# A hybrid-attention stage on one core: the compressed blocks' projections come first, their steps lie between the other units, and the two full branches run alone at the end

## What is computed

```python
def hybrid_mixer(h, w_in, gk_up, gk_bias, gla_norm, cmp_pe, cmp_w1, cmp_w2, w_out):
    q_a, k_a, v_a, lr_a, r_a, q_b, kv_b, g_b = split_cols(h @ w_in, HYB_SPLITS)
    o_a = gla_mixer(q_a, k_a, v_a, lr_a, r_a, gk_up, gk_bias, gla_norm)
    o_b = nsa_mixer(q_b, kv_b, g_b, cmp_pe, cmp_w1, cmp_w2)
    return jnp.concatenate([o_a, o_b], axis=-1).astype(h.dtype) @ w_out
...
    def compress(a, j):                      # nsa_mixer: 15 overlapping blocks of 32 tokens
        blocks = a[:, :, blk_idx] + cmp_pe[j]
        h = jax.nn.gelu(blocks.reshape(B, G, n_cmp, CMP_BLOCK * Dh) @ cmp_w1[j])
        return h @ cmp_w2[j]
...
        o = gb[..., 0:1] * o_cmp + gb[..., 1:2] * o_slc + gb[..., 2:3] * o_win
```

## Time and profile before

| | us |
|---|---|
| median of 3 runs | 2643.16 |
| the profiled execution, its own time | 2645.73 |
| its span in the trace | 2643.9 |
| projections, from the first matmul to the first score `S` of a full branch | 45.12 to 157.15 |
| attention, to the first `ul_hyb_out` | 157.15 to 260.37 |
| output product and the sum into X, about | 260.4 to 298 |

### The profile page before, as it was taken

How to read it: one execution, slowest core, us unless ns; L and a number is a source line. 1 busy time by engine, 2 the same in 40 slices (tenths; PEclk the granted TensorE clock), 3 DMA queues, 4 the chain that set the end, 5 groups by cost and what they waited for, 6 DMA issues and landing times.

```text
span 2643.9 us, 32969 instructions
## 1 busy us (share of the span) xinstructions
PE 2432.2 (92%) x13898; PEld 2108.3 (80%) x13898; DVE 1984.5 (75%) x2208; ACT 1431.7 (54%) x1594; POOL 209.3 (8%) x261
## 2 busy tenths in 40 slices
PE   4877899898889999999999999998897999897998
PEld 3756799787777888888888888887887997886997
DVE  6756777686657898888888989886666775767675
ACT  3312443464546776767676767674444653344562
POOL 1101001000000000000000000001311110221110
PEclk8886899897889999999999999999998999998999
DMA  9652678432256999999999999995224453323552
GB/s 318 216 196 88 215 271 302 158 139 81 96 182 232 348 360 347 358 348 360 352 356 337 369 338 367 342 365 191 69 96 159 164 190 134 108 76 118 195 184 77
DMA packets 263558, 608.44 MB, mean 230 GB/s; under 512 B 18472, under 2 KB 33082, under 8 KB 263402
## 3 DMA queue, kind: packets, MB, share of 16 engines
q1 hardware_dynamic: 247808, 554.39, 58.4%
q0 software_dynamic: 14640, 51.49, 5.8%
q10 hardware_dynamic: 954, 0.37, 0.1%
HBM read 605.17 MB, written 1.05 MB: 229 GB/s over the span
## 4 chain that ended last, share of the span: by engine, by line
PE 80%; DVE 10%; ACT 5%; DMA 2%; issue 1%; POOL 1%; SPq 0%; PEldq 0%; PEld 0%; DVEq 0%; ACTq 0%; POOLq 0%
PE ps L132 78%; PE ps L136 2%; DVE eb L153 1%; DMA slots<-in_hyb_mod_w 1%; DVE X L153 1%; ACT L142 1%; DMA beside<-in_dense_mod_w 1%; DVE ul_in L145 1%; DVE macc L153 1%; DVE xn L153 1%; ACT uh_ffn L139 0%; ACT eb L139 0%; ACT xn L139 0%; DVE ul_ssm_w L145 0%; DVE gate L153 0%
## 5 line engine op out<-in xcount | busy, mean ns | idle before, releaser
L145 DVE TENSOR_TENSOR ul_moe_w<-slots,uh_moe_w 128x2048 fp32r<-128x2048 f32 x334 | 762.6, 2290 | 108.7 <-ACT uh_moe_w L139 108.4
L139 ACT ACTIVATE uh_moe_w<-slots 128x2048 fp32r<-128x2048 f32 x334 | 640.2, 1917 | 215.8 <-PE ps L132 187.4
L132 PE MATMUL ps<-uh_moe_w,XGh 128*128 128x512 f32 x896 | 356.7, 398 | 3.1 <-DVE XGl L145 2.1
L132 PE MATMUL ps<-uh_moe_w,XGl 128*128 128x512 f32 x896 | 349.5, 390 | 0.0
L132 PE MATMUL ps<-ul_moe_w,XGh 128*128 128x512 f32 x896 | 349.0, 389 | 0.0
L145 DVE TENSOR_TENSOR ul_ffn<-slots,uh_ffn 128x2048 fp32r<-128x2048 f32 x62 | 142.1, 2292 | 101.1 <-ACT uh_ffn L139 101.1
L132 PE MATMUL ps<-HTf,uh_ffn 128*128 128x256 f32 x704 | 201.5, 286 | 2.8 <-DVE HTlf L145 2.8
L132 PE MATMUL ps<-HTlf,uh_ffn 128*128 128x256 f32 x704 | 201.0, 285 | 0.0
L132 PE MATMUL ps<-HTf,ul_ffn 128*128 128x256 f32 x704 | 200.9, 285 | 0.0
L132 PEld LDWEIGHTS ps<-uh_moe_w,XGh 128*128 128x128 f32 x896 | 168.3, 188 | 39.1 <-DVE XGl L145 2.2
L132 PEld LDWEIGHTS ps<-uh_moe_w,XGl 128*128 128x128 f32 x896 | 168.2, 188 | 35.8
(11 more groups left out here) (509 smaller groups left out, 5576.4 us busy)
## 6 DMA issues: line engine op xcount, KB each, us to landing
slots<-in_moe_w_gu SPq DMA_DIRECT2D x111, 2048.0 KB, 8.8
slots<-in_moe_w_down SPq DMA_DIRECT2D x56, 2048.0 KB, 7.9
slots<-in_w_up SPq DMA_DIRECT2D x20, 2048.0 KB, 7.9
slots<-in_w_in SPq DMA_DIRECT2D x14, 2048.0 KB, 8.5
slots<-in_dense_w_gu SPq DMA_DIRECT2D x10, 2048.0 KB, 9.9
slots<-in_ssm_w_in SPq DMA_DIRECT2D x10, 2048.0 KB, 8.0
slots<-in_w_down SPq DMA_DIRECT2D x10, 2048.0 KB, 7.8
slots<-in_dense_w_down SPq DMA_DIRECT2D x5, 2048.0 KB, 12.7
```

The source lines that it names most:

```text
L132: return self.e.matmul(o, lhsT, rhs, start=start, stop=stop, skip_group_check=skip) if self.e else DONE
L139: return self.e.activation(o, i, f, **kw) if self.e else DONE
L145: return self.e.tensor_tensor(o, a, b, op) if self.e else DONE
```

## The change

The units of the compressed blocks' input (`hyb_c`) come first and their first-layer weights (`hyb_w1`) are loaded third and fifth. The compressed branch leaves the woven part: its generators are created before the projections' loop and `beside` takes one step of them behind the tile and GLA piece of given steps n. Three GLA pieces move by two steps. Banks and buffers are divided anew: `mix` takes the place of `xn`, `nb0` gets its own buffer, and `bkc` (the bank of the compressed branch) has one bank. The multiplication with the gate (`facc`) moves behind the arrival of `gt`. The branches alone are woven at the end.

```diff
-    mix = c.sb("mix", [128, 2, D], ph)
+    mix = xn
...
-    units = [Unit("hyb_r", (KC, 528), slice(0, KC), slice(0, 16), False)] + row_units("hyb_r", 528, 16, 2)
+    units = column_units("hyb_c", 256, 128)
+    units += [Unit("hyb_r", (KC, 528), slice(0, KC), slice(0, 16), False)] + row_units("hyb_r", 528, 16, 2)
     units += column_units("hyb_qk", 512, 128) + row_units("hyb_v", 512, 0, 2) + column_units("hyb_q", 512, 128)
-    units += column_units("hyb_c", 256, 128) + column_units("hyb_kv", 256, 128) + column_units("hyb_kw", 280, 128)
+    units += column_units("hyb_kv", 256, 128) + column_units("hyb_kw", 280, 128)
...
-    bk1, bk2, bs = c.pool(range(4)), c.pool(range(4, 7)), c.pool([7])
-    bkc, bkb = c.pool(range(5, 7)), [c.pool(range(0, 3)), c.pool(range(3, 5))]
+    bk1, bk2, bkc, bs = c.pool(range(4)), c.pool(range(4, 6)), c.pool([6]), c.pool([7])
+    bkb = [c.pool(range(0, 3)), c.pool(range(3, 6))]
...
-    LR, R, QK, V, Q, C, KV0, KV1, GT = 0, 1, 5, 9, 13, 17, 19, 21, 23
+    C, LR, R, QK, V, Q, KV0, KV1, GT = 0, 2, 3, 7, 11, 15, 19, 21, 23
...
     def sync(e):
+        def compressing(j):
+            c.load(e, ("hyb_w1", j), io["nsa_cmp_w1"][0][j].rearrange("(i p) n -> p i n", p=128), (16, 256))
+
+        c.columns(e, "hyb_c", W, 2064, 256)
         c.columns(e, "hyb_r", W, 1024, 528)
+        compressing(0)
         c.columns(e, "hyb_qk", W, 0, 512)
+        compressing(1)
         c.columns(e, "hyb_v", W, 512, 512)
         c.load(e, "hyb_q", None, (KC, 512), heads)
-        c.columns(e, "hyb_c", W, 2064, 256)
         c.columns(e, "hyb_kv", W, 2320, 256)
         c.columns(e, "hyb_kw", W, 2576, 280)
-        for j in range(2):
-            c.load(e, ("hyb_w1", j), io["nsa_cmp_w1"][0][j].rearrange("(i p) n -> p i n", p=128), (16, 256))
...
-    Z, GATES, SCALED, STATE, INSIDE, OUTER, NORM = 6, 7, 10, 14, 17, 19, 23
+    Z, GATES, SCALED, STATE, INSIDE, OUTER, NORM = 6, 7, 12, 16, 19, 21, 25
...
-    def blocks(e, hf, compressed, rest):
-        if hf == 0:
-            yield from compressed(e)
-        else:
-            for _ in range(8):
-                yield
-        yield from rest(e, hf)
+    COMPRESSED, BLOCKS = (5, 11, 13, 14, 15, 16, 17), (21, 22, 23, 25)
+
+    def beside(n, compressed, *halves):
+
+        if n in COMPRESSED:
+            next(compressed, None)
+        if n in BLOCKS:
+            for half in halves:
+                next(half, None)
...
-        e.tensor_tensor(facc[:, :], smc[:, :], gt[:, hf, :].rearrange("p (a c) -> p c a", c=3)[:, 0, :], ALU.mult).then_inc(*v.up(("facc", hf)))
...
         ps = c.psum.of(("nsa_oc", hf))
+        e.wait_ge(*v.at("gt"))
+        e.tensor_tensor(facc[:, :], smc[:, :], gt[:, hf, :].rearrange("p (a c) -> p c a", c=3)[:, 0, :], ALU.mult).then_inc(*v.up(("facc", hf)))
...
     def tensor(e):
         c.side_banks = bs
+        small_parts = compressed_tensor(e), blocks_tensor(e, 0), blocks_tensor(e, 1)
         e.wait_ge(*v.at(("HT", 7)))
         for n in range(NU + AHEAD):
...
             gla_tensor(e, n)
+            beside(n, *small_parts)
         S.t.mark("in_end")
-        weave(branch_tensor(e, 0), branch_tensor(e, 1), blocks(e, 0, compressed_tensor, blocks_tensor), blocks(e, 1, None, blocks_tensor))
+        weave(branch_tensor(e, 0), branch_tensor(e, 1))
```

More of the change, by code:

```diff
@@ L1052, in hybrid @@
     pe2 = c.sb("pe2", [128, 2, 16], ph)
-    ph.close()
     gla_landed, nsa_landed = c.event_signal("gla_consts_landed", 16), c.event_signal("nsa_consts_landed", 16)
-    pg = c.above(86)
-    hT, hTl = c.sb("HT0", [128, KC, T], pg, R32), c.sb("HTl0", [128, KC, T], pg, R32)
-    units = [Unit("hyb_r", (KC, 528), slice(0, KC), slice(0, 16), False)] + row_units("hyb_r", 528, 16, 2)
-    units += column_units("hyb_qk", 512, 128) + row_units("hyb_v", 512, 0, 2) + column_units("hyb_q", 512, 128)
-    units += column_units("hyb_c", 256, 128) + column_units("hyb_kv", 256, 128) + column_units("hyb_kw", 280, 128)
[L1061 to L1074, removed]
+    pg = ExitStack()
     Sb = [c.sb(f"S{i}", [128, 8, 256], pg) for i in range(2)]
@@ L1079, in hybrid @@
     facb = [c.sb(f"fac{i}", [128, 8], pg) for i in range(2)]
-    small = [[c.sb(f"c{n}{i}", sh, pg) for n, sh in (("s", [128, 8, 16]), ("m", [128, 8]), ("u", [128, 8]), ("f", [128, 8]), ("p", [128, 128]), ("t", [128, 128]))] for i in range(2)]
     pg.close()
-    mh, ml = c.put(44, "mixTh", [128, 8, T], R32), c.put(52, "mixTl", [128, 8, T], R32)
+    hT, hTl = c.sb("HT0", [128, KC, T], ph, R32), c.sb("HTl0", [128, KC, T], ph, R32)
+    units = column_units("hyb_c", 256, 128)
+    units += [Unit("hyb_r", (KC, 528), slice(0, KC), slice(0, 16), False)] + row_units("hyb_r", 528, 16, 2)
+    units += column_units("hyb_qk", 512, 128) + row_units("hyb_v", 512, 0, 2) + column_units("hyb_q", 512, 128)
+    units += column_units("hyb_kv", 256, 128) + column_units("hyb_kw", 280, 128)
+    U = Units(S, "in", units, 1024, ph)
+    vT = [c.sb(f"vT{i}", [128, T], ph) for i in range(2)]
+    hid = c.sb("hid", [128, 2, 2, 2, 16], ph)
+    hx = c.sb("hx", [30, 2, 256], ph)
+    px = ExitStack()
+    xk = c.sb("xk", [128, 2, 16, 30], px)
+    px.close()
+    hy, hz = c.sb("hy", [30, 2, 256], ph), c.sb("hz", [30, 2, 256], ph)
+    kcT = c.sb("kcT", [128, 16], ph)
+    vbd = c.sb("vbd", [128, 8, 64], ph)
+    hrep = c.sb("hrep", [128, 2, 8, 16], ph)
+    vct = c.sb("vct", [128, 64], ph)
+    small = [[c.sb(f"c{n}{i}", sh, ph) for n, sh in (("s", [128, 8, 16]), ("m", [128, 8]), ("u", [128, 8]), ("f", [128, 8]), ("p", [128, 128]), ("t", [128, 128]))] for i in range(2)]
+    nb = [c.sb("nb0", [128, 2, 512], ph), Og[:, :, :, :].rearrange("p g a v -> p g (a v)")]
+    ph.close()
+    mh, ml = c.put(36, "mixTh", [128, 8, T], R32), c.put(44, "mixTl", [128, 8, T], R32)
     O = Units(S, "out", tile_units(("hyb_out", 0), 4, 1) + tile_units(("hyb_out", 4), 4, 1), 1024,
-              buffers=[c.put(at, f"u{n}_hyb_out", [128, 3, 1024], R32) for n, at in (("h", 60), ("l", 72))])
-    bk1, bk2, bs = c.pool(range(4)), c.pool(range(4, 7)), c.pool([7])
-    bkc, bkb = c.pool(range(5, 7)), [c.pool(range(0, 3)), c.pool(range(3, 5))]
+              buffers=[c.put(at, f"u{n}_hyb_out", [128, 3, 1024], R32) for n, at in (("h", 52), ("l", 64))])
+    bk1, bk2, bkc, bs = c.pool(range(4)), c.pool(range(4, 6)), c.pool([6]), c.pool([7])
+    bkb = [c.pool(range(0, 3)), c.pool(range(3, 6))]
     bt, bs2 = c.pool(range(3)), c.pool([3])
@@ L1121, in gpsimd @@
             e.dma_start(w2[:, j, :, :], io["nsa_cmp_w2"][0][j].rearrange("(c p) d -> p c d", p=128)).then_inc(*nsa_landed.up("consts"))
+        e.memset(hid[:, :, :, :, :].rearrange("p a b c d -> p (a b c d)"), 0.0).then_inc(*g.up("hid0"))
         c.follow(e, "hyb_in")
         S.g.mark("in_end")
-        S.wait_for(e, "in_end")
-        e.memset(hid[:, :, :, :, :].rearrange("p a b c d -> p (a b c d)"), 0.0).then_inc(*g.up("hid0"))
         c.follow(e, "hyb_attention")
@@ L1169, in tile_tensor @@
         U.used(n)
-        if C <= n < KV0:
+        if C <= n < LR:
             j = n - C
@@ L1233, in tile_vector @@
             c.psum.leave(("hyb_tile", n), v)
-        elif C <= n < KV0:
+        elif C <= n < LR:
             j = n - C
@@ L1437, in compressed_tensor @@
         c.side_t.step()
-        for _ in range(3):
-            yield
+        yield
         for j in range(2):
@@ L1473, in compressed_scalar @@
         e.activation(hz[:, :, :], hy[:, :, :], AF.Exp, scale=-2.0 * 0.7978845608028654).then_inc(*a.up("gelu"))
-        for _ in range(6):
+        for _ in range(4):
             yield
@@ L1758, in scalar @@
         U.split_hi(e, 1)
+        small_parts = compressed_scalar(e), blocks_scalar(e, 0), blocks_scalar(e, 1)
         for n in range(AHEAD, NU + AHEAD):
@@ L1784, in vector @@
         U.split_lo(e, 1)
+        small_parts = compressed_vector(e), blocks_vector(e, 0), blocks_vector(e, 1)
         for n in range(AHEAD, NU + AHEAD):
```

8 lines of the change are left out of this document (4 added, 4 removed).

## The result

| | before | after |
|---|---|---|
| median of 7 runs, us | 2642.9 (2632.05 to 2646.93) | 2658.42 (2653.31 to 2662.03) |
| ratio of the runs, 95% interval | | 1.006 (1.004 to 1.0081) |
| profiled execution: its time, span | 2645.73, 2643.9 | 2662.03, 2660.2 |
| first `S` of a branch | 157.15 | 215.54 |
| first `ul_hyb_out` | 260.29 | 269.06 |

The first `ul_hyb_out` before starts at 260.29; the table ahead of the prediction has it 0.08 us too late. One execution of the later run with the steps by engine and two banks took 4004.5 us at a granted clock of 0.56, where its others had 0.95; it counts in that run's median and not in its ratio.

The account below looks back on a forecast made before the run. Attention was taken as bound by chains between engines, projections by PE with DVE close behind. Projections +52 and attention -48 us gave +4, about 2650 us profiled and 2647 us median, range 2635 to 2659.

Parts of the forecast that it names:

- Two of the named signs: Profile signs in the projections: `hx` shows 6.4 to 9 us twice; second `vbd` product's bank wait is 10 us or more.
- The attention: Attention without the compressed branch: branches alone take 55 us, giving back 48 us, bounds 45 and 51.
- 1 and 2, the moved products: Compressed-branch products laid between projection units on PE: two `hx` add 13.6 us, the small ones 7.5 us.
- 3, the waits: Projections: PE waits that nothing covers, for tiles DVE must treat first, at steps 5 to 23; sum 19.2 us.
- Rival B: Projections: DVE runs ahead and waits are covered better than counted, so faster, 2635 us; chance 0.22.
- 4, the end: Projections' end: gates, whole norm, table load, `cf`/`nb` pairs and first scores before the first `S`, 13.4 against 5.5: +7.9 us.
- 5, the clock: Projections: new waits and crowded small products make about ten more us of slow PE clock, each worth half: +5 us.
- rival C: Projections' second half: clock falls throughout, six units of ten run slow, adding 8 us: 2655 us; chance 0.18.
- C's own sign: Granted clock between the first V unit and the last unit below 0.75 would decide for the slow-clock rival, chance 0.18.
- 6, the start: Projections' start: longer first unit costs 0.85 us, while `GATES` and `SCALED` chains wait 1 and 1.4 us less: -1.5 us.
- Rival D: Projections: `hyb_v` or the second `hyb_w1` loads late, each late us costing PE one: 5 us, 2652 us; chance 0.10.
- "Everything from `ul_hyb_out` on has its old length": Everything behind the hybrid stage: claimed unchanged in length; a change there would come from none of the predicted steps.

Follow-up runs that it names:

- all three edits: Changed kernel with steps placed per engine, two banks for the compressed branch plus later table preload, and the norm at step 24: 2616.76 us, ratio 0.9915.

## Why the prediction was nearly right, and where it was off

**The forecast.** It was even, +4 us, and the stage came out at +8.8 and, in the second trace, +8.3. The range held the result by 0.6 us; the forecast value was 11 us low, and "within 0.2%" was given more than it deserved. That the range held is in part luck: the stage alone would have given about 2652, and the rest of the way to its edge came from a part of the kernel that the prediction took as fixed. Two of the named signs were missed as well: the second `hx` took 10.0 us where 6.4 to 9 stood, and the wait for the bank was 8.6 us where 10 or more stood.

**The attention**, -48: measured -49.6. The account of what leaves the path was right to 2 us, as was its length alone: 53.5, predicted 55.

**1 and 2, the moved products**, 13.6 and 7.5: `hx` took 7.07 us each at full clock, 14.1; the small ones some 8, with the first `vbd` product (1.1). That product runs beside DVE's norm (201.61 to 202.7) and so lies inside the time of item 4: in the prediction's sum, as in this one, it is counted twice. Not in the prediction at all is a side product, `ones,macc`, that stood in the attention before (185.33, 1.84 us) and now stands at 194.59 between two units: 2.0 us.

**3, the waits**, 19.2: in the order of the list 2.0, 3.2, 3.3 (2.36 and 0.90), 2.1, 0.2 more for the side's `macc` (1.16, where 0.94 stood before), 1.04 twice, 3.9 and 2.6, together 19.3. Rival B, that DVE runs ahead and covers them, is refuted row by row. Its mechanism was right all the same: the run with the steps placed by engine shows that the cover can be had, but it must be written into the tables.

**4, the end**, +7.9: 13.9 us from the last turn of the gates to `S`, where I had 13.4. The cost was right, but the share was not seen: I booked it as the norm and the branch's products together, and the runs show a bare norm that puts 8.1 us between gates and `S`, where 1.1 stood, without any branch step moved, and a second bank that takes 3.4 us off this end and some 9 us off the whole stage. I had the wait for that bank as "at the slow clock 0.8 + 2.0"; what stood behind it in PE's queue, the scores, I had not followed.

**5, the clock**, +5: the second `hx` and six units of 24 matmuls ran wholly or partly at 1.2 GHz, two of them here:

```profile
151.10:155.60 4.50, 4.50 (x26) 4.40 (x25) 0.17 (x1) 0.00 (x0) 0.00 (x0) 0.62 1.02 403
...
174.00:179.20 5.20, 5.20 (x25) 5.20 (x25) 1.88 (x6) 0.00 (x0) 0.53 (x1) 0.50 0.84 281
```

Against just under 3.0 us at full clock the six lost 9.8 us in all, `hx` 3.0, small products 1.0 and the first unit of all 2.2; before, about 9.2 us were lost in the same way. The term was +6.8, a third more than I took. Five of the slow units are of the second half, where I had let two or three be slow and rival C six. C's own sign did not come: from the first V unit to the last unit the granted clock was 0.84, not below 0.75. The measured time is beyond C's 2655, but by what lies behind the stage more than by this term.

**6, the start**, -1.5: the waits for `v_g` and `Ee` are shorter by 0.7 and 1.4 us, as predicted, but the one for the side's `gate` is 0.9 us longer, and PE's first matmul came 1.9 us later. Together +0.7. The late start need not be the change's: with the same first unit it stood at 45.2 in the run with the steps by engine, and in the second trace of the kernel before at 46.3.

The terms as measured, 14.1 + 8 + 19.3 + 8.4 + 6.8 + 0.7 = 57.3; less the product counted twice and with the side product, 58.2, against the 58.4 us of the trace. Every mechanism of the sum stood. It was mis-sized in three terms of about 2 us each, all the same way: the clock (6.8 for 5), the start (+0.7 for -1.5) and the side product (2.0 for nothing); the others were within 0.6 us. The first `S` came 2.5 us behind the last place that I had named for it (213).

**Rival D**, late loads: no wait of PE for a DMA stands in the projections. Nothing of it was seen.

**"Everything from `ul_hyb_out` on has its old length"**: the step that failed, and the largest error against the time: 7.5 us in the profile and 6 to 7 in the medians. The two traces of one kernel show that I had taken for fixed what scatters by 12 us. Before a forecast of 4 us is made, the scatter of the untouched part must be known, and one trace of the kernel before doesn't give it.

## What to carry to other kernels

Work that was moved under a bound engine was hidden here only where its results were asked for one unit later than they were made: a table of steps for each engine, not one for all, turned +0.6% into -0.2% here, and with a second bank and the norm pulled ahead into -0.85%. Follow each wait for a bank to what stands behind it in the same queue: two products with one bank between them held the next stage's scores 8.6 us, and a second bank brought the first `S` 3.4 us nearer to the gates. And time a reorder apart from what it was made for: here the reorder alone lost as much as the whole change. That doesn't make it the only cause, for the losses don't add up: with the reorder kept, a second bank alone brought the stage's end back to 259.3 us.

## What was not expected of the hardware

The clock that a unit gets doesn't follow from the wait ahead of it alone. Behind the same wait of 3.12 us for `v_g`, the next 24 matmuls took 3.10 us at full clock in the run with the steps by engine and 4.47 us in the run with all three edits, where a wait of 0.24 us for `rs` came in addition. In the stretch from 575 on, the same instructions, with the same waits of 4.0 and 2.5 us ahead of the `eb,xt` products, took 10.3 us less in one execution than in another. "Half clock behind a wait" doesn't hold in every execution, and a single trace shows one case of it.

The clock column can also be wrong for a stretch. Over the first unit of the changed kernel it reads 1.00:

```profile
47.01:52.40 5.39, 5.39 (x24) 5.19 (x24) 1.43 (x2) 0.60 (x2) 0.00 (x0) 1.00 0.90 313
```

but 24 matmuls in 5.39 us is the pace of 1.2 GHz, as in the earlier trace rows at 0.50, and not the 3 us of a unit at full clock. Where the clock matters, the distance of the matmuls is the better witness.
